# Weighted queries of the mLSTM recurrence formed by GpSimd from rows spread through DRAM; GpSimd's part in differential attention; an order of rounding

## The chip, the core and the metric

One core of a Trainium2 chip runs the whole program in one launch. The metric is the device time of an execution in microseconds, as the median of several; lower is better.

## The reference

x has 1024 tokens of 1024 columns, with 256 context tokens beside them, all in float32. Two hybrid layers come first. Each normalizes, projects to attention and mLSTM columns, runs window attention and a chunked mLSTM in both directions, gates, joins the two parts, and projects back with w_out. Of the mLSTM the step over chunks matters here:

```python
dmat = jnp.where(lower, b[:, :, None] - b[:, None, :] + ii[:, None, :], -jnp.inf)
m_t = jnp.maximum(inter, jnp.max(dmat, axis=-1))
w_inter = jnp.exp(inter - m_t)
qk = einsum('ntd,nsd->nts', qq, kk) * jnp.exp(dmat - m_t[:, :, None])
num = w_inter[..., None] * einsum('nvd,ntd->ntv', C, qq) + einsum('nts,nsv->ntv', qk, vv)
den = w_inter * einsum('nd,ntd->nt', n, qq) + qk.sum(-1)
h = num / jnp.maximum(jnp.abs(den), jnp.exp(-m_t))[..., None]
C_new = a[:, None, None] * C + einsum('ns,nsv,nsd->nvd', w, vv, kk)
```

A second block then runs four mixers beside each other, an output projection and an MLP of 4096 columns. One mixer is differential attention, with 4 heads and 8 query blocks of 128:

```python
p = softmax(s, axis=-1)                      # two maps per head
w = p[:, :, 0] - lam * p[:, :, 1]
o = einsum('bhqk,bkhe->bqhe', w, v)
```

## The kernel before

All engines are programmed by hand: each gets one stream of instructions that it runs in order, and they meet at semaphores. What stands first in an engine's stream is done first. Large float32 products are made of rounded parts, hi*hi + hi*lo + lo*hi. ScalarE rounds a tile to its high part, VectorE or GpSimd subtracts it for the low part. At the start of layer 0 ScalarE rounds four pieces of a weight tile (`high_piece`) and then the two halves of the first pair of token tiles (`high`), for which TensorE's first product (L919) waits.

The recurrence (`mlstm`) has 10 steps j: 2 over context tiles, then 8 over the tiles of x. Each handles two directions d, so it consists of half-steps n = 2j + d. Layer 0 needs an output from all 20, layer 1 from the 16 with j of 2 and more. A half-step works on 4 heads of 128 columns:

- SP (`step`) loads queries and keys (512 KB, L774) and values (256 KB, L775) into a ring of two slots per direction, one step ahead. At j = 1 it also loads w_out (4 MB, L778). ScalarE and GpSimd form its high and low parts between their other work: `high_out` and `low_out` (L2301, 128x1024), eight of each, at the steps that the table `HIGH_AT` names.
- TensorE, `front`: two small matrices of gate rows, rounded and stacked (`row_hl`), are spread over 128 partitions by matmuls with a selecting matrix: row sums (L1096) and query weights (L1102), four of each; then it transposes the keys (L1108). `scores` is L1117. `back` makes the numerators (L1132 with the decayed scores, L1133 with the weighted queries q_w and the state) and the state's update.
- VectorE, `before`: the exponents' input from the row sums (L1672, four), and q_w, spread weights in PSUM times queries (L1680). `weigh` multiplies scores by decays (L1687). `denominators` waits for the numerators (m_num) and runs four operations of 128x4: L1696 copies from PSUM, L1697 takes the absolute value, L1699 the maximum, L1700 the reciprocal. Then L1709, four, renews the state.
- ScalarE: the exponential (L2065), weighted keys (L2057), and `divide` (L2078), the numerators times the reciprocal. TensorE's next numerators wait for it (m_h), as they take the same PSUM.
- GpSimd: rounds the gated attention of the first two tiles (`attended`, L2288 and L2290), adds the second direction's output to the first's at steps 1 and 6 to 9 (`join`, L2306, 128x512), and runs `low_out`.

Each engine works one half-step ahead: `before` and `weigh` of n + 1 stand ahead of the denominators of n.

In differential attention, s counts the 32 heads of all query blocks. TensorE makes the scores of two maps m in PSUM, VectorE takes the maxima (L3003), ScalarE the exponentials into SBUF with their sums (L3341), and VectorE combines: reciprocal (L3012), ratio (L3013), and L3016, p0 + ratio * p1 over 128x1024. TensorE transposes the result (`turn_p`), ScalarE takes it out of PSUM (`evacuate`), and TensorE multiplies it by the values. p0 and p1 have two buffers each. GpSimd has nothing to do there.

Of the kernel before, what the change touches and what calls it, by code (L numbers as in the profile page):

```python
# [17 lines left out]
F32 = mybir.dt.float32  # L18
# [3 lines left out]
ACT = mybir.ActivationFunctionType  # L22
# [208 lines left out]
def build(nc, A, out):  # L231

    with ExitStack() as ctx:
# [101 lines left out]
        row_hl = [rounded(f"row_hl{n}", ROWS + NTOK * n, NTOK) for n in range(2)]  # L335
# [20 lines left out]
        qk_ring = [[part(TW + 2048 * d + 1024 * u, 2 * MH, P) for u in range(2)] for d in range(2)]  # L356
        mv_ring = [[part(CST + 384 + 1032 * d + 516 * u, MH, MD + 1) for u in range(2)] for d in range(2)]
# [49 lines left out]
        prob2 = [[part(W2 + 2048 * u + 1024 * m, SEQ) for m in range(2)] for u in range(2)]  # L407
# [83 lines left out]
        inv_dram = [dram(f"inv_{l}", [NTILE, HEADS, P]) for l in range(DEPTH)]  # L491
        az_dram = [dram(f"az_{l}", [4, P, NTILE, P]) for l in range(DEPTH)]
# [30 lines left out]
        def first_block_layer(l, block, sems):  # L523
# [25 lines left out]
            def ada_sems(when, bufs):  # L549
# [37 lines left out]
            m_s, m_k, m_m, m_w, m_y, m_d, m_kw, m_qs, m_p, m_num, m_del, m_c, m_h, m_init = [sem_per_layer(n) for n in (  # L587
                "m_s", "m_k", "m_m", "m_w", "m_y", "m_d", "m_kw", "m_qs", "m_p", "m_num", "m_del", "m_c", "m_h", "m_init")]
# [51 lines left out]
            HIGH_AT = {3: (0,), 4: (1, 2), 5: (3,), 6: (4, 5), 7: (6,), 8: (7,)}  # L640
# [3 lines left out]
            def _(sp):  # L644
# [88 lines left out]
                def attention(l):  # L733
# [10 lines left out]
                    sp.dma_start(sel_raw[0:100, :, :], A["sel_hl"]).then_inc(m_sel_ld, 16)  # L744
                    for b in range(by_dma):
# [16 lines left out]
                def mlstm(l):  # L762
# [3 lines left out]
                    for u in range(2):  # L766
                        sp.wait_ge(mqk_out[u], 16 * 4)

                    def step(j, tiles, outputs, next_tile, next_outputs):
# [12 lines left out]
                def output(l):  # L782
                    nt = layer_tiles(l)
                    if l == DEPTH - 1:
                        sp.dma_start(final_g, A["final_g"]).then_inc(p_fg[l], 16)
                    sp.wait_ge(m_h[l], 2 * nt)
                    sp.wait_ge(m_del[l], 2 * NTILE)
                    sp.wait_ge(m_w[l], 2 * nt)
# [16 lines left out]
                    for t in range(2):  # L805
                        load(t, t)
                        load_in(t, t)
                    if l < DEPTH - 1:
# [53 lines left out]
            def _(pe):  # L862
# [216 lines left out]
                def mlstm(l):  # L1079
# [3 lines left out]
                    pe.wait_ge(m_high, 3)  # L1083
                    pe.wait_ge(m_rows, 2)

                    def front(n, d, tile, outputs):

                        st = qk_ring[d][n // 2 % 2]
                        pe.wait_ge(m_ld[d][n // 2 % 2], 32 * (n // 4) + 32)
# [2453 lines left out]
```

## Time and profile before

| | us |
|---|---|
| median of 3 runs | 2840.91 |
| lowest and highest run | 2833.8, 2845.3 |
| profiled execution, its own time | 2843.98 |
| span of its trace | 2842.2 |
| mean granted clock of TensorE (share) | 0.979 |

Busy time is the sum of an engine's instructions; TensorE's ends are modelled. The order of instructions on an engine is that of its stream, so an engine that waits holds back all that stands behind. A wait is put down to the semaphore that came last.

### The profile page before, as it was taken

How to read it: one execution, taken by the hardware profiler on the slowest of the kernel's cores; microseconds unless marked ns; L12 is line 12 of the kernel's file. 1: busy time of each engine (PE TensorE's matmuls, PEld its weight loads, DVE VectorE, ACT ScalarE, POOL GpSimd, SP SyncE). 2: the span in 40 equal slices, each digit the busy share in tenths (PEclk: the TensorE clock that was granted, in tenths of full speed). 3: DMA queues.
4: the chain of work that ended last, by engine and by line, in shares of the span. 5: the costliest groups of instructions: out<-in, count | busy, mean ns of one | idle time of the engine just before them, and what ended most of it. 6: DMA issues, size and time to landing. Idle time of an engine off the chain costs nothing. (4 is left out here: it accounts for less than half of the span.)

```text
span 2842.2 us, 38333 instructions
## 1 busy us (share of the span) xinstructions
PE 2704.3 (95%) x15464; PEld 2248.8 (79%) x15464; DVE 1551.3 (55%) x2466; ACT 990.6 (35%) x1846; POOL 314.1 (11%) x273
## 2 busy tenths in 40 slices
PE   6999999999999999999989989998999999999998
PEld 4789888878866798888878778755688888888886
DVE  4312565777644514757766546779644444444445
ACT  3201233655522311335645334378522211211112
POOL 0000100332431001102214400000100000000001
PEclk8999999999999999999989999989999999999999
DMA  6322222116465223321163421100401110110111
GB/s 273 103 81 81 78 83 83 24 35 227 141 236 209 85 75 82 95 74 46 32 215 116 163 96 55 45 1 1 156 1 34 56 59 30 59 59 30 59 50 76
DMA packets 135894, 248.67 MB, mean 87 GB/s; under 512 B 27106, under 2 KB 90260, under 8 KB 127936
## 3 DMA queue, kind: packets, MB, share of 16 engines
q1 hardware_dynamic: 114592, 231.83, 24.4%
q10 hardware_dynamic: 21152, 14.75, 1.6%
q8 instruction: 105, 1.72, 0.3%
q14 instruction: 45, 0.37, 0.1%
HBM read 198.24 MB, written 43.05 MB: 85 GB/s over the span
## 5 line engine op out<-in xcount | busy, mean ns | idle before, releaser
L967 PE MATMUL ps<-xn_hi_sb,ft_hi_sb 128*128 128x512 f32 (+1 forms) x720 | 263.4, 366 | 1.0 <-DVE ft_lo_sb L1423 1.0
L968 PE MATMUL ps<-xn_lo_sb,ft_hi_sb 128*128 128x512 f32 (+1 forms) x720 | 262.9, 365 | 0.0
L969 PE MATMUL ps<-xn_hi_sb,ft_lo_sb 128*128 128x512 f32 (+1 forms) x720 | 262.9, 365 | 0.0
L3160 DVE TENSOR_TENSOR arena_sb<-arena_sb,ps 128x512 f32<-128x512 f32 x256 | 173.0, 686 | 121.4 <-PE ps L2843 118.5
L919 PE MATMUL ps<-tm_hi_sb,xn_hi_sb 128*128 128x512 f32 (+2 forms) x608 | 216.3, 356 | 16.6 <-DVE xn_lo_sb L1337 8.2
L921 PE MATMUL ps<-tm_hi_sb,xn_lo_sb 128*128 128x512 f32 (+2 forms) x608 | 213.7, 351 | 0.0
L920 PE MATMUL ps<-tm_lo_sb,xn_hi_sb 128*128 128x512 f32 (+2 forms) x608 | 213.4, 351 | 0.0
L2802 PE MATMUL ps<-xn_hi_sb,w_up_hi_sb 128*128 128x512 f32 x512 | 199.4, 389 | 0.0
L2804 PE MATMUL ps<-xn_hi_sb,w_up_lo_sb 128*128 128x512 f32 x512 | 199.2, 389 | 0.0
L2803 PE MATMUL ps<-xn_lo_sb,w_up_hi_sb 128*128 128x512 f32 x512 | 199.2, 389 | 0.0
L2841 PE MATMUL ps<-w_down_hi_sb,h_hi_sb 128*128 128x512 f32 x480 | 186.7, 389 | 0.0
L2842 PE MATMUL ps<-w_down_lo_sb,h_hi_sb 128*128 128x512 f32 x480 | 186.7, 389 | 0.0
L2843 PE MATMUL ps<-w_down_hi_sb,h_lo_sb 128*128 128x512 f32 x480 | 186.7, 389 | 0.0
L967 PEld LDWEIGHTS ps<-xn_hi_sb,ft_hi_sb 128*128 128x128 f32 x720 | 136.7, 190 | 23.2 <-DVE ft_lo_sb L1423 1.4
L968 PEld LDWEIGHTS ps<-xn_lo_sb,ft_hi_sb 128*128 128x128 f32 x720 | 136.6, 190 | 21.6
L969 PEld LDWEIGHTS ps<-xn_hi_sb,ft_lo_sb 128*128 128x128 f32 x720 | 136.5, 190 | 21.7
L2026 ACT ACTIVATE arena_sb<-ps,neg_max_sb 128x640 f32<-128x640 f32 (+1 forms) x144 | 109.3, 759 | 105.5 <-DVE neg_max_sb L1590 101.6
L919 PEld LDWEIGHTS ps<-tm_hi_sb,xn_hi_sb 128*128 128x128 f32 x608 | 115.4, 190 | 35.2 <-issue 11.3
L3448 ACT ACTIVATE w_down_hi_sb<-arena_sb 128x2048 fp32r<-128x2048 f32 x15 | 28.7, 1916 | 326.4 <-DMA arena_sb<-in_w_down 326.4
L1589 DVE TENSOR_REDUCE row_max_sb<-ps 128x1 f32<-128x640 f32 (+1 forms) x144 | 111.8, 776 | 43.9 <-PE ps L1014 43.2
L1024 PE MATMUL ps<-ident_sb,arena_sb 128*128 128x128 f32 x672 | 107.4, 286 | 19.5 <-DVE arena_sb L1623 11.0
L921 PEld LDWEIGHTS ps<-tm_hi_sb,xn_lo_sb 128*128 128x128 f32 x608 | 115.2, 190 | 12.0
(422 smaller groups left out, 6113.5 us busy)
## 6 DMA issues: line engine op xcount, KB each, us to landing
arena_sb<-in_w_ft SPq DMA_DIRECT2D x44, 512.0 KB, 3.6
arena_sb<-mqk_dram SPq DMA_DIRECT2D x36, 512.0 KB, 3.3
arena_sb<-x_dram SPq DMA_DIRECT2D x33, 512.0 KB, 6.9
arena_sb<-in_w_ada SPq DMA_DIRECT2D x16, 1024.0 KB, 9.1
arena_sb<-in_w_up SPq DMA_DIRECT2D x16, 1024.0 KB, 6.6
arena_sb<-in_w_down SPq DMA_DIRECT2D x16, 1024.0 KB, 4.9
arena_sb<-in_xall SPq DMA_DIRECT2D x20, 512.0 KB, 4.9
arena_sb<-mv_dram SPq DMA_DIRECT2D x40, 256.0 KB, 4.0
```

Source lines behind the costliest of these rows:

```text
L919: pe.matmul(at, hi, tm_hi[b][:, k, :], start=k == 0, stop=False)
L920: pe.matmul(at, hi, tm_lo[b][:, k, :], start=False, stop=False)
L921: mm = pe.matmul(at, lo, tm_hi[b][:, k, :], start=False, stop=k == KT - 1)
L967: pe.matmul(to, hi, xn_hi_flat[:, k, at:at + size], start=k == 0, stop=False)
L968: pe.matmul(to, hi, xn_lo_flat[:, k, at:at + size], start=False, stop=False)
L969: mm = pe.matmul(to, lo, xn_hi_flat[:, k, at:at + size], start=False, stop=k == KT - 1)
L2802: pe.matmul(at, hi, xn2_hi[:, k, cols], start=k == 0, stop=False)
L2803: pe.matmul(at, hi, xn2_lo[:, k, cols], start=False, stop=False)
L2804: mm = pe.matmul(at, lo, xn2_hi[:, k, cols], start=False, stop=k == KT - 1)
L2841: pe.matmul(at, h_hi[u][:, k, rows], hi[:, k, cols], start=k == 0, stop=False)
L2842: pe.matmul(at, h_hi[u][:, k, rows], lo[:, k, cols], start=False, stop=False)
L2843: mm = pe.matmul(at, h_lo[u][:, k, rows], hi[:, k, cols], start=False, stop=k == FT - 1)
```

## The change

**Recurrence.** The query weights' row matrix is stored to DRAM in float32 behind the gates (two small transfers). With every half-step that has an output SP loads back its four rows of 128 values, each spread over all 128 partitions (`q_row`, 128x512, 256 KB). GpSimd multiplies them by the queries (`weigh_queries`, L2314), after the loads and after the numerators of two half-steps before, which read the same q_w. TensorE's L1102, VectorE's L1680 and the rounding of the second row matrix are gone. `HIGH_AT` names pairs at steps 3, 4 and 5. In layer 1 w_out's load is issued at j = 3 instead of j = 1; in layer 0 it stays. The load of final_g moves behind the first loads of the output stage, as q_row lies in its memory.

**Differential attention.** For the first 30 of the 32 heads VectorE makes the ratio and scales p1 in place (L3042, L3046), and GpSimd adds p1 to p0 in two halves; for the last two heads VectorE combines in halves. p0 gets a third buffer. TensorE transposes in halves, with values of earlier heads in quarters between them. ScalarE takes out the attended values before the transposed weights.

**Rounding.** At the start of layer 0 ScalarE rounds the first half of the tokens behind two pieces of the weights, and the second half behind the third.

```diff
+        q_row = [[part(42656 + 1024 * d + 512 * u, MH, P) for u in range(2)] for d in range(2)]
...
-        prob2 = [[part(W2 + 2048 * u + 1024 * m, SEQ) for m in range(2)] for u in range(2)]
+        prob2 = [[part(W2 + at, SEQ) for at in (0, 2048, 4096)], [part(W2 + at, SEQ) for at in (1024, 3072)]]
...
-            HIGH_AT = {3: (0,), 4: (1, 2), 5: (3,), 6: (4, 5), 7: (6,), 8: (7,)}
+            HIGH_AT = {3: (0, 1), 4: (2, 3), 5: (4, 5), 6: (6,), 7: (7,)}
...
+                    for d in range(2):
+                        sp.dma_start(rows_dram[l][d], row_i[32 * d:32 * d + MH, :]).then_inc(m_rows_out[l], 16)
...
-                        if j == 1:
+                            if outputs:
+                                rows = rows_dram[l][d, :, tiles[d] * P:(tiles[d] + 1) * P].unsqueeze(0).to_broadcast([P, MH, P])
+                                sp.dma_start(q_row[d][j % 2], rows).then_inc(m_ld[d][j % 2], 16)
+                        if j == (1 if nt > NX else 3):
...
-                            if not first:
-                                pe.wait_ge(m_qs[l], c)
-                            for h in range(MH):
-                                mm = pe.matmul(ps[:, 2, h * P:(h + 1) * P], sel_hl[0:100, d * MH + h, :], row_hl[1][0:100, bass.ts(tile, P)],
-                                               start=True, stop=True)
-                            mm.then_inc(m_w[l], 1)
...
-                        dve.wait_ge(m_w[l], c + 1)
-                        if not isinstance(c, int) or c >= 2:
-                            dve.wait_ge(m_num[l], c - 1)
-                        st = qk_ring[d][n // 2 % 2]
-                        dve.tensor_tensor(q_w[d], ps[:, 2, :].rearrange("p (h t) -> p h t", h=MH), st[:, 0:MH, :], ALU.mult)\
-                            .then_inc(m_qs[l], 1)
...
-                        for n in range(4):
-                            high_piece(n)
-                        high(l, 0)
+                        high_piece(0)
+                        high_piece(1)
+                        high_half(l, 0, 0)
+                        high_piece(2)
+                        high_half(l, 0, 1)
+                        high_piece(3)
...
+                    def weigh_queries(n, d, outputs):
+
+                        if not outputs:
+                            return
+                        c = n - 2 * (NTILE - nt)
+                        slot = n // 2 % 2
+                        pool.wait_ge(m_ld[d][slot], state_ld(n // 2))
+                        if c >= 2:
+                            pool.wait_ge(m_num[l], c - 1)
+                        pool.tensor_tensor(q_w[d], q_row[d][slot], qk_ring[d][slot][:, 0:MH, :], ALU.mult).then_inc(m_qs[l], 1)
...
+                        weigh_queries(2 * j + 1, 1, outputs)
+                        if j == 0:
+                            for t in range(2):
+                                attended(t, att_hi[t], att_lo[t])
+                        if next_tile is not None:
+                            weigh_queries(2 * j + 2, 0, next_outputs)
...
+                    def turn_p(s, h, half):
+                        pe.wait_ge(d_w, 2 * s + half + 1)
+                        if half == 0 and s > 0:
...
-                            turn_p(s, h)
+                            of, p, at = (b, 0, 2 * h - 4) if h >= 2 else (b - 1, 1, 2 * h)
+                            if h % 2 and of >= 0:
+                                values(of, p, at)
+                            turn_p(s, h, 0)
+                            if h % 2 == 0 and of >= 0:
+                                values(of, p, at)
+                            if of >= 0:
+                                values(of, p, at + 1)
                             if more:
                                 scores(*following, 1)
-                            if h >= 2:
-                                values(b, 0, h - 2)
-                            elif not first:
-                                values(b - 1, 1, h)
+                            turn_p(s, h, 1)
...
-                        ch.start(2 * s)
+                        ch.start(s)
                         c = recip[:, u, 2 * h + 1:2 * h + 2]
                         ch(dve, dve.reciprocal(c, l_all[:, s // 4, 2 * h + 1:2 * h + 2]))
-                        ch(dve, dve.scalar_tensor_tensor(out=row_max[:, u, h:h + 1], in0=l_all[:, s // 4, 2 * h:2 * h + 1], scalar=neg_lam[:, :], in1=c,
-                                                         op0=ALU.mult, op1=ALU.mult))
-                        p0, p1 = prob2[h % 2]
-                        dve.scalar_tensor_tensor(out=p0, in0=p1, scalar=row_max[:, u, h:h + 1], in1=p0, op0=ALU.mult, op1=ALU.add)\
-                            .then_inc(d_w, 1)
+                        dve.tensor_scalar(row_max[:, u, h:h + 1], l_all[:, s // 4, 2 * h:2 * h + 1], neg_lam[:, :], c, ALU.mult, ALU.mult).then_inc(d_ratio, 1)
+                        p0, p1 = prob2[0][s % 3], prob2[1][s % 2]
+                        dve.wait_ge(d_ratio, min(2 * s, BY_POOL + s) + 1)
+                        if s < BY_POOL:
+                            dve.tensor_scalar(p1, p1, row_max[:, u, h:h + 1], None, ALU.mult).then_inc(d_ratio, 1)
+                            return
+                        dve.wait_ge(d_w, 2 * s)
+                        for half in range(2):
+                            at = slice(SEQ // 2 * half, SEQ // 2 * (half + 1))
+                            dve.scalar_tensor_tensor(out=p0[:, at], in0=p1[:, at], scalar=row_max[:, u, h:h + 1], in1=p0[:, at],
+                                                     op0=ALU.mult, op1=ALU.add).then_inc(d_w, 1)
...
-                        if m == 0 and (not isinstance(s, int) or s >= 2):
-                            act.wait_ge(d_t, s - 1)
-                        act.activation(prob2[h % 2][m], ps_flat[:, 1024 * m:1024 * (m + 1)], ACT.Exp, bias=neg_max[:, u, 2 * h + m:2 * h + m + 1],
+                        if m == 0 and s >= 3:
+                            act.wait_ge(d_t, 2 * (s - 2))
+                        if m == 1 and s >= 2:
+                            act.wait_ge(d_w, 2 * (s - 1))
+                        act.activation(prob2[m][s % (3 - m)], ps_flat[:, 1024 * m:1024 * (m + 1)], ACT.Exp, bias=neg_max[:, u, 2 * h + m:2 * h + m + 1],
...
+                def combine(s):
+
+                    pool.wait_ge(d_ratio, 2 * s + 2)
+                    p0, p1 = prob2[0][s % 3], prob2[1][s % 2]
+                    for half in range(2):
+                        at = slice(SEQ // 2 * half, SEQ // 2 * (half + 1))
+                        pool.tensor_tensor(p0[:, at], p0[:, at], p1[:, at], ALU.add).then_inc(d_w, 1)
```

What GpSimd has in the recurrence of layer 0, from the gates' end, with the semaphores that it waits for (m_h counts divisions, w_high ScalarE's roundings of w_out). Before:

```order
L2288 CAST att_hi_sb<-arena_sb 128x512 [waits m_rows_0,a_out_0]
L2290 TENSOR_TENSOR att_lo_sb<-arena_sb,att_hi_sb 128x512 [waits p_att_0]
L2288 CAST att_hi_sb<-arena_sb 128x512
L2290 TENSOR_TENSOR att_lo_sb<-arena_sb,att_hi_sb 128x512 [waits p_att_0]
L2306 TENSOR_TENSOR arena_sb<-arena_sb 128x512 [waits m_h_0] x2
L2301 TENSOR_TENSOR w_out_lo_sb<-w_out_raw_sb,w_out_hi_sb 128x1024 [waits w_high_0] x4
L2306 TENSOR_TENSOR arena_sb<-arena_sb 128x512 [waits m_h_0] x2
L2301 TENSOR_TENSOR w_out_lo_sb<-w_out_raw_sb,w_out_hi_sb 128x1024 [waits w_high_0] x2
```

In the change, the first rows of the same place; L2314 is the product of spread rows and queries (m_num counts numerators, m_ld the loads of a direction and slot), L2294 and L2296 are `attended`:

```order
L2314 TENSOR_TENSOR arena_sb<-arena_sb 128x512 [waits m_rows_out_0,m_init_0,m_rows_0,m_ld00_0,a_out_0]
L2314 TENSOR_TENSOR arena_sb<-arena_sb 128x512 [waits m_ld10_0]
L2294 CAST att_hi_sb<-arena_sb 128x512
L2296 TENSOR_TENSOR att_lo_sb<-arena_sb,att_hi_sb 128x512 [waits p_att_0]
L2294 CAST att_hi_sb<-arena_sb 128x512
L2296 TENSOR_TENSOR att_lo_sb<-arena_sb,att_hi_sb 128x512 [waits p_att_0]
L2314 TENSOR_TENSOR arena_sb<-arena_sb 128x512 [waits m_num_0,m_ld01_0]
```

and eight rows from step 2 to the second pair of low parts, L2318 being `low_out`:

```order
L2314 TENSOR_TENSOR arena_sb<-arena_sb 128x512 [waits m_num_0,m_ld10_0]
L2314 TENSOR_TENSOR arena_sb<-arena_sb 128x512 [waits m_num_0,m_ld01_0]
L2314 TENSOR_TENSOR arena_sb<-arena_sb 128x512 [waits m_num_0,m_ld11_0]
L2314 TENSOR_TENSOR arena_sb<-arena_sb 128x512 [waits m_num_0,m_ld00_0]
L2318 TENSOR_TENSOR w_out_lo_sb<-w_out_raw_sb,w_out_hi_sb 128x1024 [waits w_high_0] x2
L2314 TENSOR_TENSOR arena_sb<-arena_sb 128x512 [waits m_num_0,m_ld10_0]
L2314 TENSOR_TENSOR arena_sb<-arena_sb 128x512 [waits m_num_0,m_ld01_0]
L2318 TENSOR_TENSOR w_out_lo_sb<-w_out_raw_sb,w_out_hi_sb 128x1024 [waits w_high_0] x2
```

Two products stand ahead of each step's low parts, each waiting for numerators, and two more follow the second low part directly; before, only joins and low parts stood there.

VectorE in differential attention, two heads. Before:

```order
L3003 TENSOR_REDUCE neg_max_sb<-ps 128x1 x2
L3012 RECIPROCAL recip_sb<-arena_sb 128x1
L3013 SCALAR_TENSOR_TENSOR row_max_sb<-arena_sb,neg_lam_sb,recip_sb 128x1
L3016 SCALAR_TENSOR_TENSOR arena_sb<-arena_sb,row_max_sb 128x1024
L3003 TENSOR_REDUCE neg_max_sb<-ps 128x1 x2
L3012 RECIPROCAL recip_sb<-arena_sb 128x1
```

In the change:

```order
L3032 TENSOR_REDUCE neg_max_sb<-ps 128x1 x3
L3041 RECIPROCAL recip_sb<-arena_sb 128x1
L3042 TENSOR_SCALAR row_max_sb<-arena_sb,neg_lam_sb,recip_sb 128x1
L3046 TENSOR_SCALAR arena_sb<-arena_sb,row_max_sb 128x1024
L3032 TENSOR_REDUCE neg_max_sb<-ps 128x1 x2
L3041 RECIPROCAL recip_sb<-arena_sb 128x1
```

The combination of two tiles, L3016, has become L3046, a product of one tile with a column; the addition stands in GpSimd's stream, two of 128x512 a head.

## Rows read from the trace of the kernel before

**Rows 1.** The page: TensorE's share of the span, and the chain that ended last
```profile
PE 2704.3 (95%) x15464; PEld 2248.8 (79%) x15464; DVE 1551.3 (55%) x2466; ACT 990.6 (35%) x1846; POOL 314.1 (11%) x273
...
PE 37%; DVE 3%; ACT 1%; issue 1%; DMA 0%; SPq 0%; ACTq 0%; DVEq 0%
```

**Rows 2.** Stretches (us; busy PE, PEld, DVE, ACT, POOL; clock): recurrence, differential attention
```profile
1456.00:1472.00 16.00, 16.00 (x147) 16.00 (x146) 13.15 (x47) 8.93 (x28) 0.00 (x0) 1.00 0.48 150
1925.00:1960.00 35.00, 28.62 (x251) 20.32 (x250) 33.17 (x43) 27.97 (x45) 0.00 (x0) 1.00 0.00 1
```

**Rows 3.** Timeline of a half-step: start us, us, engine, line, operation [idle before <-releaser]
```profile
663.77 1.13 DVE L1709 SCALAR_TENSOR_TENSOR arena_sb<-arena_sb,decay_b_sb,ps 128x129 f32<-128x129 f32 x4
664.81 1.12 DVE L1672 SCALAR_TENSOR_TENSOR arena_sb<-ps,small_sb,tri_sb 128x128 f32<-128x128 f32 x4
665.85 0.68 DVE L1680 TENSOR_TENSOR arena_sb<-ps,arena_sb 128x512 f32<-128x512 f32 x1
666.79 0.69 DVE L1687 TENSOR_TENSOR arena_sb<-ps,arena_sb 128x512 f32<-128x512 f32 x1 [0.26 <-ACT arena_sb L2065]
667.75 0.16 DVE L1696 COPY den_sb<-ps 128x4 f32<-128x4 f32 x1 [0.27 <-PE ps L1133]
668.56 1.14 ACT L2078 ACTIVATE arena_sb<-ps,den_sb 128x128 f32<-128x128 f32 x4 [0.84 <-DVE den_sb L1700]
668.65 1.12 DVE L1709 SCALAR_TENSOR_TENSOR arena_sb<-arena_sb,decay_b_sb,ps 128x129 f32<-128x129 f32 x4
```

**Rows 4.** A query-weight matmul and its count; the waits of TensorE's L1132
```profile
L1102 PE MATMUL ps<-row_hl_sb,sel_hl_sb x144: 272/275/420, 650.4 to 1524.9; 100*128 100x128 f32 x144
...
PE ps L1132 <- ACT arena_sb L2078: 10.1, 6, 1.8
```

**Rows 5.** VectorE's L1697 (min, median, max ns), and the timeline around its longest
```profile
L1697 DVE SCALAR_TENSOR_TENSOR den_sb<-den_sb x36: 161/164/2332, 658.2 to 1533.2; 128x4 f32<-128x4 f32 x36
...
704.87 4.69 POOL L2301 TENSOR_TENSOR w_out_lo_sb<-w_out_raw_sb,w_out_hi_sb 128x1024 fp32r<-128x1024 f32 x2 [7.38 <-ACT w_out_hi_sb L2083]
707.25 2.33 DVE L1697 SCALAR_TENSOR_TENSOR den_sb<-den_sb 128x4 f32<-128x4 f32 x1
...
710.02 1.14 ACT L2078 ACTIVATE arena_sb<-ps,den_sb 128x128 f32<-128x128 f32 x4 [2.64 <-DVE den_sb L1700]
711.42 0.46 PE L1132 MATMUL ps<-arena_sb 128*128 128x129 f32 x2 [1.58 <-ACT arena_sb L2078]
...
713.50 0.15 DVE L1696 COPY den_sb<-ps 128x4 f32<-128x4 f32 x1
```

**Rows 6.** GpSimd's join of two 128x512 tiles (min, median, max ns)
```profile
L2306 POOL TENSOR_TENSOR arena_sb<-arena_sb x18: 1268/1276/1294, 669.8 to 1535.1; 128x512 f32<-128x512 f32 x18
```

**Rows 7.** Layer 1, start of the recurrence: transfers issued, the wait, the clock
```profile
1428.41 0.34 SPq L778 DMA_DIRECT2D w_out_raw_sb<-in_w_out  x1
...
1445.54 1.11 PE L1096 MATMUL ps<-row_hl_sb,sel_hl_sb 100*128 100x128 f32 x4 [6.44 <-DMA arena_sb<-mv_dram]
...
1445.50:1452.00 6.50, 6.46 (x31) 6.46 (x31) 2.57 (x7) 1.75 (x5) 0.00 (x0) 0.50 0.35 115
```

**Rows 8.** Timeline of one head in differential attention
```profile
1939.15 0.16 DVE L3012 RECIPROCAL recip_sb<-arena_sb 128x1 f32<-128x1 f32 x1
1939.60 1.29 DVE L3016 SCALAR_TENSOR_TENSOR arena_sb<-arena_sb,row_max_sb 128x1024 f32<-128x1024 f32 x1
1940.81 2.35 DVE L3003 TENSOR_REDUCE neg_max_sb<-ps 128x1 f32<-128x1024 f32 x2
1942.06 1.11 ACT L3341 ACTIVATE arena_sb<-ps,neg_max_sb 128x1024 f32<-128x1024 f32 x1 [0.57 <-DVE neg_max_sb L3003]
1943.30 0.16 DVE L3012 RECIPROCAL recip_sb<-arena_sb 128x1 f32<-128x1 f32 x1
```

**Rows 9.** VectorE: a 128x1024 tile of SBUF times a column
```profile
1731.67 0.81 DVE L2947 TENSOR_SCALAR arena_sb<-arena_sb,small_sb 128x1024 f32<-128x1024 f32 x1
```

**Rows 10.** TensorE's first product of layer 0 and its wait
```profile
44.05 0.77 PE L919 MATMUL ps<-tm_hi_sb,xn_hi_sb 128*128 128x512 f32 x1 [7.26 <-DVE xn_lo_sb L1337]
```

More of the change, by code:

```diff
@@ L333, in build @@
         mqk_st = [part(ACC + 1292 + NTOK * u, NTOK) for u in range(2)]
-        row_hl = [rounded(f"row_hl{n}", ROWS + NTOK * n, NTOK) for n in range(2)]
+        row_hl = rounded("row_hl", ROWS, NTOK)
         sel_raw, sel_hl = part(ROWS + 4 * NTOK, 2 * MH, P), rounded("sel_hl", ROWS + 4 * NTOK, 2 * MH, P)
@@ L491, in build @@
         inv_dram = [dram(f"inv_{l}", [NTILE, HEADS, P]) for l in range(DEPTH)]
+        rows_dram = [dram(f"rows_{l}", [2, MH, NTOK]) for l in range(DEPTH)]
         az_dram = [dram(f"az_{l}", [4, P, NTILE, P]) for l in range(DEPTH)]
@@ L638, in second_visit, with state_ld @@
                 return j == NC - 1 or j >= NC + NX // 2
-            HIGH_AT = {3: (0,), 4: (1, 2), 5: (3,), 6: (4, 5), 7: (6,), 8: (7,)}
+            HIGH_AT = {3: (0, 1), 4: (2, 3), 5: (4, 5), 6: (6,), 7: (7,)}
+            def state_ld(j):
+                with_outputs = [i for i in range(j % 2, j + 1, 2) if layer_tiles(l) > NX or i >= NC]
+                return 32 * (j // 2 + 1) + 16 * len(with_outputs)
             @block.sync
@@ L2631, in scores, with values @@
                         mm.then_inc(d_s[m], 1)
[L2633 to L2635 removed]
+                    def turn_p(s, h, half):
+                        pe.wait_ge(d_w, 2 * s + half + 1)
+                        if half == 0 and s > 0:
                             pe.wait_ge(d_t_act, s)
[L2637 to L2638 removed]
+                        for n in range(4 * half, 4 * half + 4):
+                            mm = pe.transpose(ps[:, 4 + half, (n % 4) * P:(n % 4 + 1) * P], prob2[0][s % 3][:, n * P:(n + 1) * P], ident[:, :])
                         mm.then_inc(d_t, 1)
[L2641 to L2643 removed]
+                    def values(b, p, quarter):
+                        if quarter == 0:
                             pe.wait_ge(d_t_act, 4 * b + 2 * p + 2)
@@ L2646, in values @@
                                 pe.wait_ge(d_y, b)
-                        for n in range(4 * half, 4 * half + 4):
+                        for n in range(2 * quarter, 2 * quarter + 2):
                             for g in range(2):
@@ L2689, in attention @@
                         group_mean(dw_acc, j, mu_mm)
-                    for half in range(2):
-                        values(NX - 1, 1, half)
+                    for quarter in range(4):
+                        values(NX - 1, 1, quarter)
                 def group_mean(src, n, done):
@@ L3510, in _ @@
                     root("1", t)
+                def combine(s):
[4 more added lines that the diff above has]
+                        pool.tensor_tensor(p0[:, at], p0[:, at], p1[:, at], ALU.add).then_inc(d_w, 1)
                 spatial_norm()
+                for s in range(BY_POOL):
+                    combine(s)
                 for c in range(2):
```

94 lines of the change are left out of this document (45 added, 49 removed).

## The prediction

> **What bounds the kernel now.** The page comes first. TensorE is busy for 2704.3 of 2842.2 us (95%), and GpSimd for 11% [rows 1]: work that leaves TensorE or VectorE for GpSimd pays only where the old engine ends the wait of a stage. So the stages come next, by busy time in windows. In the recurrence of layer 1, 16.00 us of 16.00 are TensorE's, with 147 matmuls, 0.109 us each [rows 2]; a half-step (one tile, one direction) has 44 of them, 4.8 us, and VectorE's state update starts 4.88 us after the one before, 663.77 to 668.65 [rows 3]. That is the period now. In differential attention VectorE is busy for 33.17 of 35 us and TensorE for 28.62 [rows 2]: VectorE's chain is the period there, 4.15 us a head (1939.15 to 1943.30) [rows 8].
>
> Two other chains of the recurrence lie close to 4.88. VectorE's own: denominators 0.90 (667.75 to 668.65), state 1.04, decay input to weighing 1.98 (664.81 to 666.79), weighing 0.69, together 4.6 [rows 3]. And the loop in which numerators wait for the division of the half-step before: 0.81 from the copy L1696 to the division [rows 3], 1.40 to the numerators (710.02 to 711.42), 2.08 to the next copy [rows 5], together 4.29.
>
> What a reader must see is the third view, L1697. It takes 161 ns at the least and 164 in the median, but 2332 at most, and that one stood beside GpSimd's rounding of w_out, which ran from 704.87 for two instructions of 2.35 us [rows 5]. This 128x4 operation reads two operands in SBUF. The large VectorE operations of the same half-steps with one operand in PSUM keep their 0.68 us [rows 3]. I read it as: VectorE's two-operand steps on SBUF wait until the GpSimd instruction under way has ended. After the long one the numerators L1132 stood 1.58 us for the division; all such waits are 10.1 us in six places [rows 4], four of them, 6.6 us, at the steps with two roundings. The Trainium skill, SBUF — State Buffer, "Who interferes with whom", says the same: such a VectorE operation and a GpSimd one share a port pair, and the one that starts first keeps it for its instruction. It speaks against this change.
>
> **Recurrence.** Removed are 144 matmuls L1102 [rows 4] (four a half-step, 0.44 us) and 36 VectorE products L1680 of 0.68 us. TensorE then needs 4.4 us a half-step. VectorE's chain stays 4.6, because the product stood in the time in which the exponential was awaited (L1687 waited 0.26 for ScalarE behind it) [rows 3]. Without collisions the period would be 4.60, 0.28 less.
>
> But each of the 36 products is now a GpSimd instruction of 1.28 us [rows 6], and it waits for m_num, the very count that releases the denominators of the half-step two before. L1696 and the product start together; L1697, about 0.3 us later, waits for the other 0.96. The loop becomes 4.29 + 0.96 = 5.25 us, 0.37 more than now. That holds for 12 half-steps (steps 0 to 2 and 8 in layer 0, 2 and 8 in layer 1): **+4.4**.
>
> Roundings of w_out now come in pairs at steps 3, 4 and 5 of both layers. As in [rows 5], L1697 meets the second part and waits 2.17 (2.33 less 0.16). New is that the next product has been released and queues behind it: it takes the gap, and L1699 waits for up to another 1.2. The half-step takes 4.29 + 2.17 + 1.2 = 7.66, its partner 5.25; the step 12.9 where two half-steps now take 9.76. Six times 3.15: **+19.0**. The four pairs of before go: **-6.6**. Steps 6 and 7 have joins and one rounding beside the products; I put 5.25 twice and half of a 1.28 met once, 11.2 for 9.76, four times 1.4: **+5.6**. The last step has no products ahead: 4 half-steps at 4.60, **-1.1**. The recurrence: **+21.3**.
>
> Three edits with it are covered. The rows loads bring 256 KB more per half-step, 1 MB in 5 us; the windows moved 150 GB/s with the DMA engines at 0.48 [rows 2], so a third more bytes fits, and the loads are issued a step ahead. The stores of the rows are two small transfers under attention. A rounding on VectorE and one on GpSimd less lie under TensorE's attention. If the loads came late, each half-step would wait by what is missing; that is the upper end.
>
> **w_out's load in layer 1** is issued at 1428.41, ahead of the loads of step 2, and TensorE stood 6.44 us for them, then ran 6.5 us at granted clock 0.50, 1.2 GHz instead of 2.4 [rows 7]. So the stall costs 6.44 and about 3.2. Issued at step 3 instead, 4 MB stands ahead of the loads of step 4, which are due one step (some 10 us) later; most of the stall moves there. Bounds: the whole goes (-10), or the same stall and a late first rounding (+3). I take **-3**, near the upper one, since the transfer is as long as before.
>
> **Differential attention.** The combination with one column (1939.60 to 1940.81, 1.21 us) becomes a scaling of one tile; the nearest row took 0.81 [rows 9]. The chain is 0.45 + 0.81 + 2.49 (1940.81 to 1943.30) = 3.75 for 4.15 [rows 8], 0.40 less. The additions on GpSimd, two of 1.28, end 2.6 us after the scaling, before the next one 3.75 later. TensorE's second scores now stand behind the turn of half 0, which waits for scaling and first addition; for every other head also behind two quarters of values. I put 0.2 for those heads, 0.1 in the mean. 31 heads times 0.30: **-9.3**. Bounds 0 (all given back) and -14 (0.45 a head: TensorE's 28.62 of 35 would allow that).
>
> **Rounding order.** TensorE's first product stood 7.26 us for the low part of a half [rows 10]; ScalarE now rounds that half two pieces earlier, about 2 us. **-2**, between 0 and -4.
>
> **Sum.** 21.3 - 3 - 9.3 - 2 = +7.0 on the profiled execution's 2843.98: 2851.0. That execution is 3.07 above the median of 2840.91, so 2848 against the median. A measurement tells 0.5% (14.2 us) from no change: the borders are 2826.7 and 2855.1.
>
> **Rivals.**
> Slower, by the clock. In a half-step of 7.66 us TensorE works 4.4 and stands 3.2. After 6.44 us standing it ran at 1.2 GHz for 6.5 us [rows 7], a loss of 3.2; after 1.58 [rows 5] nothing such shows. 3.2 lies between. If it decides for the low level, six steps lose 3 more each: 2848 + 18 = 2866. Chance 0.18.
> Faster, no collision. GpSimd's product starts later than the copy by more than the three small operations last, or its reads are short enough to let them pass; then the period is 4.60: 36 times 0.28 is -10.1, pairs wait as now in six places for four (+3.3), and with -14.3 from the other parts it gives -21.1, 2820. For it: L1697 keeps 164 ns in the median although joins and roundings run beside it. Against it: joins start after the division, not at the denominators. Chance 0.20.
> Differential attention gains nothing. The scaling has one tensor operand in SBUF but may run in the fast form; if it and GpSimd's additions shut one another out, the scaling waits for an addition whenever it comes less than 2.6 us after the last scaling, and each addition whenever it meets a scaling; up to 0.4 a head, all of the gain: 2857. The same section of the Trainium skill names VectorE's two-port modes among the operations that hold the pair; no row of before shows the two together. Against it stands the 1.1 us between the end of the additions and the next scaling. Chance 0.12.
>
> **Chances.** The forecast 0.50; of it 0.44 within 0.5%, 0.02 faster, 0.04 slower (if loads come late or the queue adds more than one product). The clock rival is slower (0.18), the third half within and half slower (0.06 each), the second faster. That makes faster 0.22, same 0.50, slower 0.28. The range takes in the forecast with the low ends of its parts (2848 less 10 for w_out and less of the roundings' price, 2829) and reaches to the clock rival with 2 us above, 2868; only the second rival is left out.
>
> **What would show it.** In the profile after: L1697 and L1699 with medians near 1 us in place of 0.16, and waits of TensorE's L1132 for the division several times 10.1 us, longest at steps 3 to 5; starts of the state update about 5.25 apart in steps 0 to 2. A granted clock under 1 behind those steps speaks for the first rival; medians of 0.16 and starts 4.6 apart for the second; a head of 4.15 and scalings over 1 us for the third. The wait of 6.44 at step 2 of layer 1 should be gone, and one appear at step 4. Wrong I am if the recurrence of layer 0 gets shorter.

## The result, and the profile after

The changed kernel takes 2853.65 us in the median of 13 runs (2847.16 to 2860.8), the kernel before 2840.91: ratio 1.0045, 95% interval 1.0033 to 1.0057. It is slower by 12.7 us; the forecast was 7 more, 2848, in a range of 2829 to 2868, and lies below the interval, which is 9.4 to 16.2 us. The profiled execution's span is 2850.9 us, 8.7 more than before. Ratios are taken from fast executions alone; the medians of the ninth and the tenth run also count one slow execution each (3819.58 and 3040.53 us).

Dated by the same instruction in both traces, the 8.7 us are made of these: TensorE's first product comes 1.7 us earlier; recurrence of layer 0, from the first row sums to the first product of the output, takes 113.6 us for 104.9; from the output of layer 0 to that of layer 1, 8.4 us more, of which the recurrence, from its first transposed keys on, is 10.0, and what lies ahead of it 1.6 less; differential attention, from the first reciprocal to the last, 131.7 us for 137.1. Between the output of layer 1 and differential attention 2.5 us go, and 1.6 come back behind it.

**The page and the denominators.** The first line is the page's. The others are the operations of the denominators and GpSimd's products (min, median, max ns), L1699, L1701 and L2314 in the changed kernel; they answer to [rows 1] and [rows 5].

```profile
PE 2697.9 (95%) x15320; PEld 2237.8 (78%) x15320; DVE 1534.7 (54%) x2430; ACT 991.2 (35%) x1846; POOL 430.4 (15%) x365
L1699 DVE SCALAR_TENSOR_TENSOR den_sb<-den_sb x36: 161/164/2326, 655.4 to 1548.2; 128x4 f32<-128x4 f32 x36
L1701 DVE TENSOR_TENSOR den_sb<-den_sb,small_sb x36: 161/164/1198, 656.7 to 1548.4; 128x4 f32<-128x4 f32 x36
L2314 POOL TENSOR_TENSOR arena_sb<-arena_sb x36: 1253/1269/1290, 648.0 to 1542.5; 128x512 f32<-128x512 f32 x36
```

TensorE is busy for 6.4 us less than before, VectorE for 16.6 less (its long denominators counted as busy), and the kernel is slower: neither engine's sum says it. The medians of L1699 and L1701 are those of before; what has changed stands in single half-steps.

**A plain half-step** in layer 0 (start us, us; timeline). It answers to [rows 3].

```profile
655.24 0.16 DVE L1698 COPY den_sb<-ps 128x4 f32<-128x4 f32 x1 [1.07 <-PE ps L1141]
655.35 1.27 POOL L2314 TENSOR_TENSOR arena_sb<-arena_sb 128x512 f32<-128x512 f32 x1 [1.01 <-PE ps L1141]
655.44 1.21 DVE L1699 SCALAR_TENSOR_TENSOR den_sb<-den_sb 128x4 f32<-128x4 f32 x1
656.68 0.16 DVE L1701 TENSOR_TENSOR den_sb<-den_sb,small_sb 128x4 f32<-128x4 f32 x1
...
660.57 0.15 DVE L1698 COPY den_sb<-ps 128x4 f32<-128x4 f32 x1
```

L1141's end releases copy and product together. L1699 starts 0.09 us after the product and ends 0.03 after it: 1.21 us for 0.16. The next copy comes 5.33 later.

**A pair of roundings**, step 3 of layer 0, the same view. It answers to [rows 5].

```profile
694.30 4.68 POOL L2318 TENSOR_TENSOR w_out_lo_sb<-w_out_raw_sb,w_out_hi_sb 128x1024 fp32r<-128x1024 f32 x2 [6.90 <-ACT w_out_hi_sb L2091]
...
696.49 0.15 DVE L1698 COPY den_sb<-ps 128x4 f32<-128x4 f32 x1
...
696.67 2.32 DVE L1699 SCALAR_TENSOR_TENSOR den_sb<-den_sb 128x4 f32<-128x4 f32 x1
...
698.94 2.48 POOL L2314 TENSOR_TENSOR arena_sb<-arena_sb 128x512 f32<-128x512 f32 x2
699.03 1.19 DVE L1701 TENSOR_TENSOR den_sb<-den_sb,small_sb 128x4 f32<-128x4 f32 x1
700.25 0.18 DVE L1702 RECIPROCAL den_sb<-den_sb 128x4 f32<-128x4 f32 x1
...
703.95 0.15 DVE L1698 COPY den_sb<-ps 128x4 f32<-128x4 f32 x1
```

L1699 waits for the second part, then the queued product takes the gap (698.94) and L1701 waits for it. The second of the two products doesn't hold the reciprocal L1702, which reads one operand. The half-step is 7.46 long.

**TensorE's waits** (total, times, longest) and stretches of low clock (us; busy PE, PEld, DVE, ACT, POOL; then the clock, the DMA engines' share, GB/s). They answer to [rows 4], [rows 7].

```profile
PE ps L1140 <- ACT arena_sb L2086: 32.4, 20, 3.5
...
PE ps L1110 <- DMA arena_sb<-rows_dram: 6.5, 3, 4.7
```

```profile
712.00:718.00 6.00, 3.53 (x16) 3.56 (x17) 3.74 (x11) 2.89 (x9) 2.02 (x2) 0.64 0.30 89
1467.00:1474.00 7.00, 5.14 (x24) 5.14 (x25) 1.82 (x5) 1.75 (x5) 1.28 (x1) 0.57 0.93 280
1486.00:1492.00 6.00, 5.94 (x28) 5.97 (x29) 2.44 (x10) 3.07 (x10) 0.00 (x0) 0.51 0.00 0
...
1868.00:1883.00 15.00, 15.00 (x39) 8.55 (x39) 8.22 (x14) 8.74 (x14) 5.01 (x4) 0.50 0.01 2
```

The waits for the division are 32.4 us in 20 places for 10.1 in six. Behind four of the six pairs TensorE stood 3.45 us, and behind three of these four (at 714.5, 1486 and 1513) it then ran at 1.2 GHz for a while; there the half-step is 9.2 long instead of 7.1 to 7.5. The stall for w_out is still there: three waits of 6.5 us in all, the longest 4.7 with the low clock of 1467 behind it, at step 4 instead of step 2.

**Differential attention**, two heads (timeline). It answers to [rows 8].

```profile
1941.74 0.16 DVE L3041 RECIPROCAL recip_sb<-arena_sb 128x1 f32<-128x1 f32 x1 [0.24 <-ACT arena_sb L3378]
...
1945.40 0.17 DVE L3041 RECIPROCAL recip_sb<-arena_sb 128x1 f32<-128x1 f32 x1
...
1949.45 0.16 DVE L3041 RECIPROCAL recip_sb<-arena_sb 128x1 f32<-128x1 f32 x1 [0.24 <-ACT arena_sb L3378]
...
1949.96 0.76 DVE L3046 TENSOR_SCALAR arena_sb<-arena_sb,row_max_sb 128x1024 f32<-128x1024 f32 x1
...
1950.79 2.51 POOL L3554 TENSOR_TENSOR arena_sb<-arena_sb 128x512 f32<-128x512 f32 x2 [1.54 <-DVE arena_sb L3046]
...
1953.63 0.75 DVE L3046 TENSOR_SCALAR arena_sb<-arena_sb,row_max_sb 128x1024 f32<-128x1024 f32 x1
```

The heads take 3.66 and 4.05 in turn, 3.86 in the mean for 4.15. The additions end at 1953.30, 0.33 us before the next scaling.

### The profile page after: what moved, and what is told of

It is laid out like the page before. It is cut to its first block and busy times, and to the rows that moved or that the text cites. A ratio compares the mean times of both kernels' runs of the same rounds, so it can differ in the third digit from the quotient of the medians.

```text
span 2850.9 us, 38172 instructions
## 1 busy us (share of the span) xinstructions
PE 2697.9 (95%) x15320; PEld 2237.8 (78%) x15320; DVE 1534.7 (54%) x2430; ACT 991.2 (35%) x1846; POOL 430.4 (15%) x365
## 5 line engine op out<-in xcount | busy, mean ns | idle before, releaser
L3195 DVE TENSOR_TENSOR arena_sb<-arena_sb,ps 128x512 f32<-128x512 f32 x256 | 173.0, 686 | 121.4 <-PE ps L2872 118.6
L933 PE MATMUL ps<-tm_hi_sb,xn_hi_sb 128*128 128x512 f32 (+2 forms) x608 | 216.4, 356 | 14.7 <-DVE tm_lo_sb L1330 6.6
L981 PEld LDWEIGHTS ps<-xn_hi_sb,ft_hi_sb 128*128 128x128 f32 x720 | 136.7, 190 | 23.2 <-DVE ft_lo_sb L1431 1.4
L3534 POOL TENSOR_TENSOR stat_sb<-stat_sb,minus_half_sb 128x1 f32 x22 | 17.1, 779 | 846.0 <-DVE stat_sb L2901 845.9
L933 PEld LDWEIGHTS ps<-tm_hi_sb,xn_hi_sb 128*128 128x128 f32 x608 | 115.4, 190 | 33.4 <-issue 9.3
```

The costliest lines, as they stand in the source:

```text
L933: pe.matmul(at, hi, tm_hi[b][:, k, :], start=k == 0, stop=False)
L981: pe.matmul(to, hi, xn_hi_flat[:, k, at:at + size], start=k == 0, stop=False)
```

## The experiments

My theory: the loss is the denominators' waits, since two operands in SBUF wait for a GpSimd instruction under way; behind a pair the queue of products adds a second wait. Rivals: the product or its loads come late and the long denominators only fill a wait; the loss comes from differential attention; the low clock makes it. Each run was timed in rounds beside the kernel before; the interval of such a ratio is 3 to 6 us on either side, and that of the difference of two ratios 5 to 8. Runs one to four, five to eight and nine to twelve are three groups, each beside its own executions of the kernel before; runs of different groups are compared by their ratios.

**The parts apart.** The edits are those of the change itself: the first run has its recurrence part (rows, products, table, w_out's load) and nothing of the other two, the second only the other two.

> The kernel before with the recurrence part of the change alone (rows through DRAM, GpSimd's products, the new table of roundings, w_out's load at step 3 in layer 1). Theory: this part holds all of the loss, and the other two parts give some of it back. The two profiles put recurrence of layer 0 at 8.7 us more, what follows up to the output of layer 1 at 8.4 more, so 16 to 21 us above the kernel before, ratio 1.006 to 1.0075. Rival, that the loss comes from differential attention or from a shift of the whole: below 10 us.

> The other two parts without the recurrence part. Theory: 6 us from differential attention and 2 from the rounding order, so 8 us faster than before (6 to 11), ratio 0.997. Rival, that GpSimd's additions cost VectorE what the scaling saves: 2 us faster and no more.

Measured: 2866.62 against 2845.47, ratio 1.0074 (1.0055 to 1.0093), and 2835.27, ratio 0.9963 (0.9949 to 0.9977). So +21 and -10.5 us, together +10.6 for the 12.7 of the whole. All of the loss is in the recurrence part, and differential attention is not where it comes from.

**The denominators with one operand in SBUF.** The third run (`least` holds exp(-m_t), `by_head` two rows of den, in the shape of the numerators; the first removed line is shortened):

```diff
-ch(dve, dve.tensor_copy(den[:, d, 0, :]..., num[:, :, :, MD]))
-ch(dve, dve.scalar_tensor_tensor(out=den[:, d, 1, :], in0=den[:, d, 0, :], scalar=-1.0, in1=den[:, d, 0, :], op0=ALU.mult, op1=ALU.max))
-ch(dve, dve.tensor_tensor(den[:, d, 2, :], den[:, d, 1, :], cols[:, 2, tile, 32 * d:32 * d + MH], ALU.max))
+ch(dve, dve.tensor_tensor(by_head[0], num[:, :, :, MD], least, ALU.max))
+ch(dve, dve.scalar_tensor_tensor(out=by_head[1], in0=num[:, :, :, MD], scalar=-1.0, in1=by_head[0], op0=ALU.mult, op1=ALU.max))
```

> The changed kernel, with the denominators' operations rewritten so that each reads one operand in PSUM: max(num, c), then max(-num, that), in place of copy, absolute value and maximum; one operation fewer, same values. Theory (two operands in SBUF wait for a GpSimd instruction under way): no operation of the denominators longer than 0.2 us, half-steps of 4.4 to 4.6 us everywhere, waits of the numerators for the division under 5 us in all; some 26 us less than the changed kernel, 10 to 16 less than before, about 2827. Rival (the product itself comes late, or the loads of the rows do, and the long denominators only fill a wait): period stays 5.3, time within 6 us of the changed kernel's 2854.

Measured: 2829.62, ratio 0.9942 (0.9928 to 0.9956), 16 us under the kernel before and some 29 under the changed one. The two operations in its trace, and TensorE's waits:

```profile
L1700 DVE TENSOR_TENSOR den_sb<-ps,small_sb x36: 151/152/165, 656.7 to 1530.0; 128x4 f32<-128x4 f32 x36
L1701 DVE SCALAR_TENSOR_TENSOR den_sb<-ps,den_sb x36: 161/161/164, 656.9 to 1530.2; 128x4 f32<-128x4 f32 x36
```

```profile
PE ps L1110 <- DMA arena_sb<-rows_dram: 11.8, 3, 7.5
...
PE ps L1140 <- POOL arena_sb L2315: 10.5, 6, 1.8
```

The longest of 72 operations took 165 ns, beside the same 36 products and 16 parts as in the changed kernel. Plain half-steps are 4.43 apart. The edit also takes one operation out of the chain, but the fourth run, which keeps all four, has plain half-steps just as short (4.43 to 4.51), so it isn't that. That decides for the theory: the products were not late, they stood in the way. What is left are two other waits: numerators for products behind a pair (10.5 us) and TensorE for loads (11.8 us).

**The product a little later.** In the fourth run the product is released by the reciprocal:

```diff
-                            pool.wait_ge(m_num[l], c - 1)
+                            pool.wait_ge(m_inv[l], c - 1)
```

> The changed kernel, with GpSimd's product released by the reciprocal (m_inv) instead of the numerators (m_num), so about 0.8 us later. Theory: products no longer meet the denominators; plain half-steps fall from 5.30 to about 4.6, and behind a pair of roundings only one wait of 2.2 us is left instead of 2.2 and 1.2, about 6.5 instead of 7.5. 12 times 0.7 and 6 to 10 times 1.0: 14 to 18 us less than the changed kernel, about 2838. Rival (a late product is what costs): longer than the changed kernel by 0.8 a half-step, 2870 or more.

Measured: 2850.74, ratio 1.0018 (1.0006 to 1.0029), 7.7 us under the changed kernel by the ratios, half of what I expected. A plain half-step and a pair:

```profile
659.08 0.16 DVE L1699 SCALAR_TENSOR_TENSOR den_sb<-den_sb 128x4 f32<-128x4 f32 x1
659.80 1.27 POOL L2314 TENSOR_TENSOR arena_sb<-arena_sb 128x512 f32<-128x512 f32 x1 [3.50 <-DVE den_sb L1702]
663.59 0.16 DVE L1699 SCALAR_TENSOR_TENSOR den_sb<-den_sb 128x4 f32<-128x4 f32 x1
...
709.58 2.25 DVE L1699 SCALAR_TENSOR_TENSOR den_sb<-den_sb 128x4 f32<-128x4 f32 x1
...
711.87 1.19 DVE L1701 TENSOR_TENSOR den_sb<-den_sb,small_sb 128x4 f32<-128x4 f32 x1
...
713.41 1.27 POOL L2314 TENSOR_TENSOR arena_sb<-arena_sb 128x512 f32<-128x512 f32 x1 [0.38 <-DVE den_sb L1702]
714.70 0.46 PE L1140 MATMUL ps<-arena_sb 128*128 128x129 f32 x2 [2.79 <-POOL arena_sb L2314]
```

Plain half-steps are right: L1699 at 0.16, 4.51 apart. At pairs I was wrong twice. One product had been released already by the half-step before, so it still held L1701; and the next, now behind the reciprocal, made the numerators wait (23.2 us in ten places in this trace). The rival of the late product has its place here, but only behind pairs.

**The table alone**, the fifth run:

```diff
-            HIGH_AT = {3: (0, 1), 4: (2, 3), 5: (4, 5), 6: (6,), 7: (7,)}
+            HIGH_AT = {3: (0,), 4: (1, 2), 5: (3,), 6: (4, 5), 7: (6,), 8: (7,)}
```

> The changed kernel with the kernel before's table of roundings: pairs at steps 4 and 6, single parts at 3, 5, 7 and 8. Theory (each pair costs 2 to 3 us more than a step with one part, by the starts of the denominators 12.6, 14.8 and 11.6 us apart at pairs and 10.6 at single parts): one pair fewer per layer, one single part more late in the recurrence, 3 to 5 us less than the changed kernel, about 2850 to 2854 in this measurement's terms (before 2845). Rival (the table is worth nothing, since a part costs the same wherever it stands): within 1.5 us of the changed kernel.

Measured: 2850.28 against 2842.25, ratio 1.0036 (1.0022 to 1.0051). Its distance to 1.0045 is 2.5 us with intervals that overlap: this doesn't settle what the table is worth. In the trace after the pairs' steps in layer 0 take 12.6, 14.8 and 11.6 us and those with one part 10.6. But from the first to the last reciprocal of the denominators, both layers together, this run's trace has 198.8 us and that of the changed kernel 198.8 too: the pair at step 6 takes 12.5 us here, the last half-step of layer 0 5.6 for 4.3, and a load holds TensorE for 1.5. So whether the old table is worth anything stays open.

**The old recurrence without the wait.** The sixth run has the recurrence of before with the third run's denominators, and the change's other two parts.

> The recurrence of before (TensorE spreads the query weights, VectorE multiplies) with the one-operand denominators of the third run, and the change's differential attention and rounding order. Theory: the 10.1 us of TensorE's waits at pairs go, plain half-steps stay 4.88 as TensorE sets them: 8 to 10 us less than the second run, 2826 or so, within 5 us of the third run. Rival (the denominators' waits were hidden before): as the second run, 2835.

Measured: 2826.65 against 2842.25, ratio 0.9948 (0.9933 to 0.9963); the second run had 0.9963. The waits of L1132 for the division, 10.1 us in six places, are 2.3 in two. By the times the gain is 4 us, less than the 8 to 10 that I expected, and the two intervals overlap. The traces show more: from the first to the last reciprocal, both layers together, 164.2 us for 173.0 before (and in the second run), 8.7 less. By the starts of before, 701.90, 707.06 and 713.50, a pair costs 0.28 and 1.56 more than 4.88, some 7 us for four; the rest lies at each layer's end. So the recurrence gains what I expected in one trace, and why the times gain only half of it stays open.

**What was left of the new recurrence.** The seventh run is the third with each low part a step later, one behind each product:

```diff
+                        parts = HIGH_AT.get(j - 1, ())
+                        for k in parts[0:1]:
+                            low_out(k)
                         if next_tile is not None:
                             weigh_queries(2 * j + 2, 0, next_outputs)
...
-                        for k in HIGH_AT.get(j, ()):
+                        for k in parts[1:2]:
                             low_out(k)
```

> As the third run, with each low part of w_out in GpSimd's stream one step later and behind one product instead of two in a row at the step's end. Theory: in the third run the numerators waited 1.8 us, six times, for a product that stood behind two low parts; a product of 1.28 and one part of 2.36 fit a half-step of 4.43, so these 10.5 us go: 8 to 11 us less than the third run, about 2820. Rival (GpSimd is then late for ScalarE's parts, or the stall moves to the last step): within 3 us of the third run.

Measured: 2814.75 against 2842.25, ratio 0.9908 (0.9891 to 0.9926), 9.7 us under the third run by the ratios. No wait of L1140 for GpSimd is left in its trace; the waits for loads are.

The eighth run is the third with w_out in four loads:

```diff
-                        if j == (1 if nt > NX else 3):
+                        if j in (1, 2, 3, 4):
                             sp.wait_ge(a_out[l], nt)
-                            sp.dma_start(w_out, A["w_out"][l]).then_inc(p_w[l], 16)
+                            k = 2 * (1, 2, 3, 4).index(j)
+                            sp.dma_start(w_out[:, k:k + 2, :], A["w_out"][l][:, k:k + 2, :]).then_inc(p_w[l], 16)
```

ScalarE's roundings (`high_out`) wait for the transfer that brings their piece.

> As the third run, with w_out loaded in four transfers of 1 MB behind the loads of steps 1, 2, 3 and 4, in both layers, instead of one of 4 MB. Theory: the three waits of TensorE for loads of the rows (11.8 us, the longest 7.5) and the low clock behind them go, less the part that layer 1's start keeps: 8 to 15 us less than the third run, about 2818. Rival (the transfers' sum is what counts, 2 MB of loads and 1 MB of w_out in 8.9 us): waits spread over steps 2 to 5, within 4 us of the third run.

Measured: 2816.49, ratio 0.9914 (0.9896 to 0.9931), 8 us under the third run. TensorE's waits for the rows' loads are 5.2 us where they were 11.8:

```profile
PE ps L1111 <- DMA arena_sb<-rows_dram: 5.2, 4, 2.3
```

The ninth run has all three edits.

> The changed kernel with one-operand denominators, one low part per product and w_out in four loads. Theory: the two gains over the third run are of different waits (10.5 us for GpSimd's products, 8 to 12 us for the loads and the clock behind them) and add up: 32 to 38 us less than before, ratio 0.987 to 0.989. Rival (both shorten the same steps 3 to 5, and TensorE's own 4.43 a half-step is reached by either): 26 to 29 us less, as each alone.

Measured: 2807.35 against 2840.34, ratio 0.9875 (0.9854 to 0.9896): 35 us under the kernel before, and 19 under the third run, for 9.7 and 8 alone. The two gains add up within the intervals.

```profile
L1701 DVE TENSOR_TENSOR den_sb<-ps,small_sb x36: 150/152/165, 655.6 to 1504.4; 128x4 f32<-128x4 f32 x36
...
PE ps L1111 <- DMA arena_sb<-rows_dram: 3.9, 5, 1.6
```

**Does the new recurrence pay at all?** The tenth run gives the old one the same two helps.

> The recurrence of before with one-operand denominators and w_out in four loads, and the change's other two parts. Theory: the sixth run less the wait of 6.2 us at step 2 of layer 1 and the low clock behind it, 20 to 24 us less than before; the new recurrence then earns the rest, 0.44 us in each of 36 half-steps (16 us at the most, 10 to 14 with what is lost at the start). Rival (the old recurrence does as well once nobody waits): within 4 us of the ninth run.

Measured: 2819.89, ratio 0.9925 (0.9906 to 0.9945). The ninth is 14 us shorter, with 8 on either side; from the first to the last reciprocal the traces of the two layers have 154.1 us for 164.4. The ninth also has another order of the low parts, which the tenth lacks, but the tenth's pairs cost it nothing (4.95 and 4.81 for 4.88 twice). So without collisions the move to GpSimd pays, by an amount near the 16 us of the 144 matmuls.

**w_out's load in layer 1 alone**, the eleventh run:

```diff
-                        if j == (1 if nt > NX else 3):
+                        if j == 1:
```

> The changed kernel with w_out's load in layer 1 back at step 1. My prediction had the move at 3 us less; the trace after shows waits for the rows' loads of 6.5 us with a low clock behind the longest, as long as the one of before. Theory: the stall is only moved, within 2 us of the changed kernel. Rival (the move pays as forecast, or more, since the loads of three transfers a direction are hit harder at step 2): 3 to 10 us more.

Measured: 2853.56 against 2840.34, ratio 1.0040 (1.0027 to 1.0054), the same as the changed kernel. The one wait for loads in layer 1 is then 6.1 us at step 2. Moving the load moves the stall; splitting it shortens it, to 5.2 us in the eighth run and 3.9 in the ninth, and in the tenth no such wait is left.

**The collision put back.** The twelfth run is the ninth with the changed kernel's denominators.

> The ninth run with the changed kernel's denominators (two operands in SBUF, copy, absolute value, maximum), nothing else. Theory: 0.87 us come back in each half-step whose numerators release a product and up to 2.2 where a low part is under way: 36 half-steps, 25 to 35 us more than the ninth run, about the kernel before's time. Rival (with parts and products apart there is room to wait): under 10 us more.

Measured: 2847.88, ratio 1.0025 (1.0013 to 1.0037), 43 us above the ninth by the ratios, more than the 25 to 35 that I expected.

```profile
L1700 DVE SCALAR_TENSOR_TENSOR den_sb<-den_sb x36: 161/1186/2377, 653.5 to 1546.6; 128x4 f32<-128x4 f32 x36
L1702 DVE TENSOR_TENSOR den_sb<-den_sb,small_sb x36: 161/164/2264, 654.8 to 1546.8; 128x4 f32<-128x4 f32 x36
...
695.82 1.27 POOL L2315 TENSOR_TENSOR arena_sb<-arena_sb 128x512 f32<-128x512 f32 x1
695.87 1.25 DVE L1700 SCALAR_TENSOR_TENSOR den_sb<-den_sb 128x4 f32<-128x4 f32 x1
697.05 2.34 POOL L2319 TENSOR_TENSOR w_out_lo_sb<-w_out_raw_sb,w_out_hi_sb 128x1024 fp32r<-128x1024 f32 x1
697.15 2.26 DVE L1702 TENSOR_TENSOR den_sb<-den_sb,small_sb 128x4 f32<-128x4 f32 x1
```

With a part behind each product, the denominators meet the product with one operation and the part with the other, 3.2 us in one half-step. The form of two operations of four columns a half-step costs more than the 16 us of matmuls that the recurrence part takes away.

## Why the prediction was right, and where it was off

The direction and the mechanism were right; the sum was 5.7 us short of the measured time. Some errors in it cancel: the recurrence is 18.7 us more in the trace (8.7 and 10.0), for 18.3 with the load, but out of other terms than I had put.

- **What bounds it, and the wait for GpSimd:** right. The third and twelfth runs show it both ways, by the same edit taken away and put back. By the Trainium skill's rule (SBUF — State Buffer, "Who interferes with whom") the side that starts first holds the shared pair of ports for its instruction; the rows at 655.35 and, in the twelfth run, 695.82 agree. The same section says that a VectorE instruction with at most one input in SBUF, outside the two-port modes, does not contend with GpSimd; 165 ns at most in the third run agrees.
- **Plain half-steps, 5.25:** 5.33, 5.20 and 5.24 in steps 0 to 2 of layer 0. The 12 that I counted were fewer: beside joins one of two was 4.5. The first eight half-steps of layer 0 are together 2.2 us longer than at 4.88 each.
- **Pairs, 7.66 and 5.25:** 7.46 and 5.14 at the first, 7.06 and 4.5 at the third. The second was 9.19 long, as were two of layer 1 (low clock). The six steps together cost 22.2 us more, for 19.0.
- **The clock rival** (0.18) came true in half of its places: behind three of six pairs TensorE fell to 1.2 GHz, about 2 us each. This is a part of what the sum lacks; I had it in all six places or in none. In other traces with the same denominators it came oftener: in the first run's behind four pairs of six, in the eleventh's behind all six.
- **Steps 6 and 7, 11.2:** 10.6 in three of four and 10.7 in one of layer 1: +3.4 in place of +5.6.
- **w_out's load, -3:** this step failed. The eleventh run gives 0 with about 5 us on either side, and the trace waits of 6.5 us with a low clock behind, for 6.44. I had named "the same stall" as a bound and taken more.
- **Recurrence as a whole, +18.3 with the load:** +21 in the first run (15.6 to 26.5), 18.7 in the changed kernel's trace.
- **Differential attention, -9.3:** 5.4 in the trace. The chain was right (3.66 and 4.05, in the mean 3.86; I had 3.85), and the heads with queries among them gained 0.27 each. The loss is in the second head, 7.64 us for 5.33: TensorE ran at 0.50 up to 1883 us, and before only up to 1862, which is 1874.5 in the later time of the changed kernel. The other heads gained 7.8 us in all, 0.26 each for my 0.30. That second head is not a price of the change: eleven other runs have the same code here, and in ten of their traces it took 4.8 to 6.1 us. The stage took 127.8 to 131.8 us in the twelve traces with the new code, 130.4 in the median, and 137.1 and 138.3 in the two with the old. The second run has -10.5 with the rounding.
- **Rounding, -2:** L933 starts at 42.31, 1.74 earlier than in [rows 10].
- **The third rival** (scaling and additions shut each other out) wasn't tried: scalings take 753 to 756 ns and additions 1264 to 1286, and in the heads shown the two never run at once, so nothing here tells what they would do to each other. The room between them is 0.33 us there and not 1.1; I had left out the 0.8 us of the scaling itself.
- **A sign that was wrong:** I expected medians near 1 us for L1699. They are 0.16, as only 17 of the 36 are long; with L1701 half of the half-steps, 18, have a long operation. The starts and the waits showed it, the median didn't.

## What to carry to other kernels

Before work is given to GpSimd, look which of VectorE's operations with two operands in SBUF the same event releases: here such an operation of 0.16 us took 1.2 beside a product and 2.3 beside a rounding, and what it costs is its place in the loop, not its size. Often the operand can be read in PSUM instead of a copy of it, which is one operation less besides; here that turned a change of +12.7 us into -16, and with roundings and loads spread out into -35. A large load that stalls the loads behind it is split, not moved.

## What the runs showed that I had not expected

- The better order for one wait was the worse for the other. With two parts in a row (changed kernel) 28 operations of the denominators are longer than 0.2 us, and they take 33.9 us more than at 0.16 each; with parts and products apart (twelfth run) they are 33, and take 39.6 more. The seventh's order and the four loads together gave 19 us without collisions (ninth against third run) and 6 with them (twelfth against the changed kernel).
- In the changed kernel's trace, behind the same wait of 3.45 us, TensorE's clock fell in three cases of four: the window behind 714.5 has 0.64, the one behind 701.87 (704 to 710) has 1.00. In the six traces with GpSimd's products and the old denominators (changed kernel, first, fourth, fifth, eleventh and twelfth run), numerators waited 3.35 to 3.46 us in 21 places, and the clock was at 1.2 GHz within 2 us of the wait's end in 20 of them. After waits of 2.3 to 2.9 us it fell in six of twelve, and after the 1.58 of before it stayed at 1.00.
- The stall behind a 4 MB load in layer 1 did not go away by moving it. TensorE's waits for loads there are 6.1 to 6.4 us with the load at step 1 (before, second, sixth and eleventh run), 6.5 to 9.5 with the load at step 3 (changed kernel, first, third, fourth, fifth and seventh run). In layer 0, where the 4 MB load stands at step 1 in all of these, they are between nothing and 3.0 us.
